# Two transformer blocks in one program: adaLN's shift left out of the first layer's h and added to k, v and the first queries as rows

## The reference, cut to what matters

```python
shift, scale, gate = jnp.split(jax.nn.silu(c) @ ada_w[l] + ada_b[l], 3, axis=-1)
h = rmsnorm(x, norm_g[l]) * (1.0 + scale[:, None]) + shift[:, None]      # the same for ctx with c_ctx
q, k, v, up, uf, g = split_proj(h @ w_in[l])
q = apply_axial_rope(rmsnorm(q.reshape(B, N, N_HEADS, HEAD_DIM), q_norm_g[l]), cos, sin)   # k alike
att = latent_attention(q, k, v, kc, vc)        # 8 query heads, 2 key heads of 128; keys of ctx and x
out = merge_branches(att, up, uf, g, pool_w[l], pool_scale[l], fourier_w[l], w_out[l])
x_new = x + gate[:, None] * out
```

## Time and profile before

| | |
|---|---|
| median of 3 runs | 2457.78 us (2452.79 to 2459.43) |
| the profiled execution's own time | 2455.74 us |
| its span | 2453.9 us |
| PE busy | 2318.9 us, 94% |
| DVE busy | 1288.8 us, 53% |
| ACT busy | 1044.1 us, 43% |
| HBM read over the span | 428.37 MB |
| mean granted TensorE clock | 0.976 of 2.4 GHz |

### The profile page before, as it was taken

The page is one execution under the profiler, slowest core; times in us unless marked ns, Lnnn a source line. Parts: engine busy times, 40 slices in busy tenths (PEclk is TensorE's granted clock), DMA queues, the critical chain, the costliest instruction groups (busy, mean ns, idle before and its releaser), DMA issues.

```text
span 2453.9 us, 30582 instructions
## 1 busy us (share of the span) xinstructions
PE 2318.9 (94%) x12135; PEld 1857.9 (76%) x12135; DVE 1288.8 (53%) x2110; ACT 1044.1 (43%) x1596; POOL 196.6 (8%) x237
## 2 busy tenths in 40 slices
PE   5889999999999997899998988989999999999998
PEld 2467777777777665678887877868888888888887
DVE  2444533132332254445666786556765666566664
ACT  2232333342321263445544555445543555345543
POOL 1000100000010122100012014120000000000001
PEclk8989999999999998999999999989999999999999
DMA  9764343435655583534555554545555555566652
GB/s 367 284 246 163 131 140 108 138 104 172 240 172 172 183 302 114 188 105 141 186 172 155 175 186 129 173 135 187 184 189 185 184 186 187 190 188 188 195 187 89
DMA packets 347021, 436.66 MB, mean 178 GB/s; under 512 B 13848, under 2 KB 269280, under 8 KB 345984
## 3 DMA queue, kind: packets, MB, share of 16 engines
q1 hardware_dynamic: 341376, 413.19, 51.1%
q0 software_dynamic: 3408, 16.38, 1.8%
q10 hardware_dynamic: 2096, 5.15, 0.6%
HBM read 428.37 MB, written 6.29 MB: 177 GB/s over the span
## 4 chain that ended last, share of the span: by engine, by line
PE 84%; DVE 5%; ACT 4%; DMA 3%; POOL 2%; issue 2%; SPq 0%; ACTq 0%; POOLq 0%; DVEq 0%
PE ps L1142 31%; PE ps L1143 16%; PE ps L1137 5%; PE ps L1139 5%; PE ps L1138 5%; PE ps L1123 4%; PE ps L1125 4%; PE ps L1124 4%; PE ps L1104 3%; ACT SPL L1320 2%; DMA RAW<-in_w_in_dram 2%; DVE SPL L1546 1%; PE ps L1187 1%; PE ps L1204 1%; DMA RAW<-in_ada_w_dram 1%
## 5 line engine op out<-in xcount | busy, mean ns | idle before, releaser
L1142 PE MATMUL ps<-HS,SPL 128*128 128x512 f32 x3456 | 1230.0, 401 | 18.0 <-POOL HS L1998 17.0
L1546 DVE TENSOR_TENSOR SPL<-RAW,SPL 128x1024 fp32r<-128x1024 f32 x592 | 725.7, 1231 | 667.2 <-ACT SPL L1320 665.6
L1143 PE MATMUL ps<-HS,SPL 128*128 128x256 f32 x3456 | 968.8, 280 | 0.0
L1320 ACT ACTIVATE SPL<-RAW 128x1024 fp32r<-128x1024 f32 x592 | 621.8, 1057 | 538.1 <-PE ps L1143 349.6
L1142 PEld LDWEIGHTS ps<-HS,SPL 128*128 128x128 f32 x3456 | 654.3, 189 | 182.3 <-POOL HS L1998 17.6
L1143 PEld LDWEIGHTS ps<-HS,SPL 128*128 128x128 f32 x3456 | 656.6, 190 | 2.1 <-issue 1.9
L1123 PE MATMUL ps<-SPL,HS 128*128 128x512 f32 x576 | 248.0, 430 | 22.3 <-ACT XT L1362 8.6
L1125 PE MATMUL ps<-SPL,HS 128*128 128x512 f32 x576 | 228.3, 396 | 0.0
L1124 PE MATMUL ps<-SPL,HS 128*128 128x512 f32 x576 | 228.1, 396 | 0.0
L1137 PE MATMUL ps<-HS,SPL 128*128 128x512 f32 x512 | 212.3, 415 | 1.2 <-DVE HS L1702 1.2
L1139 PE MATMUL ps<-HS,SPL 128*128 128x512 f32 x512 | 200.5, 392 | 0.0
(11 more groups left out here) (251 smaller groups left out, 1542.0 us busy)
## 6 DMA issues: line engine op xcount, KB each, us to landing
RAW<-in_w_in_dram SPq DMA_DIRECT2D x208, 512.0 KB, 5.7
RAW<-in_ada_w_dram SPq DMA_DIRECT2D x192, 512.0 KB, 4.9
RAW<-in_ffn_w_up_dram SPq DMA_DIRECT2D x192, 512.0 KB, 3.5
RAW<-in_w_out_dram SPq DMA_DIRECT2D x96, 512.0 KB, 4.5
RAW<-in_ffn_w_down_dram SPq DMA_DIRECT2D x96, 512.0 KB, 3.3
x_spill<-XT POOLq DMA_DIRECT2D x2, 2048.0 KB, 15.1
XT<-x_spill POOLq DMA_DIRECT2D x1, 4096.0 KB, 16.1
MM<-in_x_dram ACTq DMA_DIRECT2D x2, 1024.0 KB, 10.6
```

The source lines that it names most:

```text
L1142: mm(PS[b][:, :], wr, hh, start=k == 0, stop=False, skip_group_check=True)
L1143: m = mm(PS[b][:, 256:512], wl, hh[:, 0:256], start=False, stop=k == KT - 1, skip_group_check=True)
L1320: act(SPL[:, (n - 1) % NSPL, 0, :], raw_of(i), ACT.Copy).then_inc(s_hi, 1)
L1546: tt(w[:, 1, :], raw_of(s["i"]), w[:, 0, :].bitcast(F32), ALU.subtract).then_inc(s_lo, 1)
```

## The change

Layer 0 reads k, v and the first queries from an h without the shift (`bare`), which needs only the scale groups. `start(u)` has 8 adaLN chunks (40 chunks in all with k,v instead of 72), and in u = 0 each second of them pops six steps. The shift groups come with q0 (`go_on(u)`), and `shift_h` then adds the shift to h in place (DVE, ACT, DVE), ahead of q1 and all that follows. The rows of k,v and q0 are copied from PSUM into BARE, in MM. What the shift contributes to them, shift @ w_in, is computed by itself: the w_in columns of k,v and of q0 are loaded once more as 16 chunks of form "ada", multiplied by ADA's shift columns, copied, spread over the 128 rows by a matmul with a selecting matrix (`shift_rows`, SPREAD, loaded by `select_in`), and added by DVE. q0's norm steps are made after that, behind q1's in the list, and the low list of attention rows starts there. `mixed` places pairs of `left` chunks after every chunk of the output stage and after every two elsewhere. AHEAD is 7 (from chunk 40 on). In layer 1 q0 and q1 have side 2, their norm steps go to the front of `hi` and through bank 7, and q1's rows no longer flush the list.

```diff
...
-AHEAD = 5
+AHEAD = 7
...
+        BARE = [MV[:, i, 8:16, :].rearrange("p k n -> p (k n)").rearrange("p (t c) -> p t c", t=4) for i in range(2)]
+        SPREAD = MV[:, 1, 7, :].rearrange("p (v n) -> p v n", v=2)
...
-            while at["taken"] < min(len(queue), at["pos"] + (START_AHEAD if at["pos"] < 72 else at["ahead"])):
+            while at["taken"] < min(len(queue), at["pos"] + (START_AHEAD if at["pos"] < 40 else at["ahead"])):
...
-                    pop_side(2 if c.group.side == 2 and c.kc % 2 == 0 else 0)
+                    pop_side(c.group.side if c.kc % 2 == 0 else 0)
...
-        def mixed(main, left):
+        def mixed(main, left, every=2):
             seq = []
-            for c in main:
-                seq.append(c)
-                if len(seq) % 4 == 2:
-                    seq.extend(left[:2])
-                    del left[:2]
+            for i in range(0, len(main), every):
+                seq.extend(main[i:i + every] + left[:2])
+                del left[:2]
             return seq
...
+        def shift_h(k, s, bare, done, used):
+            y = {}
+            def s0():
+                y["slot"], last = take()
+                y["h"] = put("h0", l=0, k=k, s=s, slot=y["slot"], shifted=True, last=[ada_ready[0, k // 4], bare[k, s], *last])["n"]
+            def s1():
+                y["h"] = put("h1", l=0, k=k, s=s, slot=y["slot"], scaled=y["h"], last=[used])["n"]
+            def s2():
+                h = put("h2", l=0, k=k, s=s, slot=y["slot"], hi=y["h"], again=0)
+                give(y["slot"], (s_h2, h["n"]))
+                done[k, s] = (s_h2, h["n"])
+            return [s0, s1, s2]
...
-                if both or x.get("qs_used"):
+            def rows_out(banks, width, queries=False):
+                if queries and not both:
+                    while x.get("norms_left"):
+                        hi.pop(0)()
+                elif x.get("qs_used"):
                     flush(hi)
                 x["qs_used"] = True
-                s = put("rows_out", l=l, banks=banks, width=width, last=[multiplied(), *x["qs"]], a=count.get("qa", 0), d=count.get("qd", 0))
-                x["qs"] = []
+                while "tab" not in x:
+                    hi.pop(0)()
+                last, x["qs"] = [multiplied(), *x["qs"]], []
+                return copy_rows(banks, width, [lv.QS[:, i, 0:width] for i in range(len(banks))], last)
...
+            def bare_out(which):
+                def f():
+                    x["bare"][which] = copy_rows([0, 1, 2, 3], 512, [BARE[which][:, i, :] for i in range(4)], [multiplied()])
+                return f
+            def shift_rows(which):
+                def after():
+                    slot, last = take()
+                    s = put("ada_out", slot=slot, last=[multiplied(), *last])
+                    bank_last[6] = [(s_adaE, s["n"])]
+                    if not hi:
+                        hi.append(idle)
+                    hi.insert(1, lambda: add(slot, s["n"]))
+                def add(slot, out):
+                    while "scr_a" not in x:
+                        hi.pop(0)()
+                    s = put("shift_rows", which=which, slot=slot, out=out, ready=x["bare"][which], last=x["scr_a"], after=use(4, 5))
+                    n = 4 * s["n"]
+                    give(slot, (s_sp, s["n"]))
+                    bank_last[4], bank_last[5] = [(s_srow, n)], [(s_srow, n)]
+                    if which == 0:
+                        hi.extend(staged([norm_item(i, 2, 1, tt, (s_srow, n - 3 + i), lv.KTr[:, :, i * 128:(i + 1) * 128], BARE[0][:, i, 0:256])
+                                          for i, tt in enumerate(TILES)]))
+                    else:
+                        hi.extend(staged([norm_item(i, 4, 0, tt, (s_srow, n - 3 + i), MV[:, tt[0], 0:4, tt[1] * 128:(tt[1] + 1) * 128], BARE[1][:, i, :])
+                                          for i, tt in enumerate(TILES)]) + [lambda: start_units(0)])
+                return group("ada", "shift", W, (1024, 0)[which], [6], after)
...
-                    ready = rows_out(banks, 512)
-                    hi.extend(staged([norm_item(i, 4, 0, tt, ready[i], MV[:, tt[0], 4 * g:4 * g + 4, tt[1] * 128:(tt[1] + 1) * 128])
-                                      for i, tt in enumerate(lv.tiles)]))
-
-                    def start_units():
-                        us.extend(unit(hd, *tt) for hd in range(4 * g, 4 * g + 4) for tt in lv.tiles)
-                        if g == 0 and both:
-                            low.extend([unit_row] * (2 * len(us) + 3))
-                    hi.append(start_units)
+                    ready = rows_out(banks, 512, True)
+                    steps = staged([norm_item(i, 4, 0, tt, ready[i], MV[:, tt[0], 4 * g:4 * g + 4, tt[1] * 128:(tt[1] + 1) * 128])
+                                    for i, tt in enumerate(lv.tiles)]) + [lambda: start_units(g)]
+                    if both:
+                        hi.extend(steps)
+                    else:
+                        x["norms_left"] = True
+                        hi[:0] = steps + [lambda: x.update(norms_left=False)]
                 return f
+            def start_units(g):
+                us.extend(unit(hd, *tt) for hd in range(4 * g, 4 * g + 4) for tt in lv.tiles)
+                if g == 0 and both:
+                    low.extend([unit_row] * (2 * len(us) + 3))
...
-            kv = group("tm", ("kv", l), W, 1024, [0, 1, 2, 3], kv_out, TILES)
-            q0 = group("tm", ("in", l), W, 0, qb[0], q_out(0, qb[0]), lv.tiles)
-            q1 = group("tm", ("in", l), W, 512, qb[1], q_out(1, qb[1]), lv.tiles)
+            kv = group("tm", ("kv", l), W, 1024, [0, 1, 2, 3], bare_out(0) if both else kv_out, TILES)
+            q0 = group("tm", ("kv", l), W, 0, qb[0], bare_out(1), TILES) if both else group("tm", ("in", l), W, 0, qb[0], q_out(0, qb[0]), lv.tiles, 1 if both else 2)
+            q1 = group("tm", ("in", l), W, 512, qb[1], q_out(1, qb[1]), lv.tiles, 1 if both else 2)
...
-                cs = ada_group(0, 4 + u, 2) + ada_group(0, u, 2)
+                cs = ada_group(0, 4 + u, 2 if u else 6)
                 after_ada = cs[-1].then
                 def start_h():
                     after_ada()
                     if u == 3:
                         put("spill", last=[multiplied()])
-                    hi.extend(staged([tile_h(0, k, s, x, h) for k in range(4 * u, 4 * u + 4) for s in range(2)])
-                              + ([load_tables, tables, load_dft] if u == 3 else []))
+                    hi.extend(staged([tile_h(0, k, s, x, bare) for k in range(4 * u, 4 * u + 4) for s in range(2)])
+                              + ([lambda: put("select_in"), load_tables, tables, load_dft] if u == 3 else []))
                 cs[-1].then = start_h
-                return cs[:12] + kv[2 * u - 2:2 * u - 1] + cs[12:] + kv[2 * u - 1:2 * u] if u else cs
+                return cs[:4] + kv[2 * u - 2:2 * u - 1] + cs[4:] + kv[2 * u - 1:2 * u] if u else cs
+            def go_on(u):
+                c = q0[2 * u + 1]
+                after_q = c.then
+                def add_shift():
+                    while (0, u) not in ada_ready:
+                        hi.pop(0)()
+                    used = multiplied()
+                    hi.extend(staged([shift_h(k, s, bare, h, used) for k in range(4 * u, 4 * u + 4) for s in range(2)]))
+                    if after_q:
+                        after_q()
+                c.then = add_shift
+                cs = ada_group(0, u, 2)
+                return cs[:4] + q0[2 * u:2 * u + 1] + cs[4:] + [c]
...
-                main = [c for u in range(4) for c in start(u)] + kv[6:8], q0 + q1 + gp + gf + gates
+                main = ([c for u in range(4) for c in start(u)] + kv[6:8] + [c for u in range(4) for c in go_on(u)]
+                        + mixed(q1, shift_rows(0) + shift_rows(1), 1)), gp + gf + gates
...
-        lay_out(mixed(outs0, left))
+        lay_out(mixed(outs0, left, 1))
...
+                elif kind == "shift_rows":
+                    for sm, v in new((s_sel, 16)):
+                        e.wait_ge(sm, v)
+                    e.wait_ge(s_adaE, s["out"])
+                    for src in range(2):
+                        m = mm(PS[4 + src][:, :], SPREAD[:, src, :], T(s["slot"]), start=True, stop=True, skip_group_check=True)
+                    m.then_inc(s_sp, 1)
...
+                    if s["shifted"]:
+                        stt(T(s["slot"])[:, 0:256], HX(0, k, src, 0).bitcast(F32), shift(0, k, src), HX(0, k, src, 1).bitcast(F32), ALU.add, ALU.add).then_inc(s_h0, 1)
+                        continue
...
-                    stt(HX(0, k, src, 1), T(s["slot"])[:, 0:256], shift(0, k, src), HX(0, k, src, 0).bitcast(F32), ALU.add, ALU.subtract).then_inc(s_h2, 1)
+                    tt(HX(0, k, src, 1), T(s["slot"])[:, 0:256], HX(0, k, src, 0).bitcast(F32), ALU.subtract).then_inc(s_h2, 1)
+                elif kind == "shift_rows":
```

(21 more changed lines are left out.)

76 lines of the change are left out of this document (45 added, 31 removed).

## The result

The changed kernel takes 2501.44 us (median of 4 runs, 2495.56 to 2505.73) against 2458.56 us of the kernel before (4 runs). The ratio is 1.0173, interval 1.0156 to 1.019: 42.9 us slower, where 12 us faster was predicted.

What follows compares the result with a forecast made beforehand. TensorE, busy 94% of the span, was taken as the bound. Start -13.6, attention burst +9.8 and layer 1 -8 summed to -11.8 us, 2446 us (own range 2440 to 2453; eight times in ten 2428 to 2464).

Steps and rivals of the forecast that it cites:

- (a): Layer 0's start: first wide matmul at 47.5 us, 18.8 us sooner, with half as many adaLN chunks ahead.
- (b): Layer 0, first wide matmul to end of k,v: ends at 106 us, the 8.3 us spill wait gone.
- (c): Layer 0's q0 with the shift's 32 adaLN chunks: 61.3 us of PE plus 7 of waits, ending at 174.5 us.
- (d): Layer 0's q1 with 16 shift chunks: 54.4 us of work plus 6 of waits, ending at 235 us.
- Seven chunks ahead where no adaLN chunk stands changes nothing: Deeper split look-ahead where no adaLN chunk stands: priced at 0, as four splits are the limit.
- (e): Layer 0's pool group: second spread 1.7, q0's transposes 2.3 and 4 us of waits, reaching 243 us.
- (f): Start's like-for-like correction for gate chunks (8 us) and attention rows (11 us) now later: 262 against 275.6, -13.6 us.
- Attention burst: Layer 0's third gate group: 13 attention rows run in a row without wide matmuls, +9.8 us (bounds 0 to 45).
- Layer 1: Layer 1's start: q1 -12 us from shorter head-transpose waits, q0 +4, together -8 us (bounds -18 to +2).
- The adaLN chunks moved into the output stage are the same work: 0: Layer 0's output stage: a pair and wide chunk take 6.4 us of PE against 4.3 of loads, no change.
- Rival (2): No change, some 2456 us: table waits, norm waits and slower loads give back 15.5 us at full; chance 0.25 with another.
- Rival (1): Slower: attention burst without overlap, deciding the sign from 1.7 us idle a row; 2475 us at 3 us; chance 0.15.

Runs made afterwards that it cites:

- e8: Changed kernel with the gate group needing heads 0 and 1 two groups later, splits five chunks ahead up to chunk 136 and seven after: 2454.5 us.
- e13: e7 with the splits seven chunks ahead from chunk 40 up to chunk 136, five behind it: 2480.4 us.
- e1: Changed kernel with the splits five chunks ahead instead of seven: 2471.4 us, ratio to before 1.006.
- e7: e5 with 16 adaLN chunks moved back from layer 0's output stage to layer 1's start: 2440.3 us, ratio to before 0.9923.
- e9: e7 with layer 1's own steps undone as well: 2448.1 us.
- e2: Changed kernel with the gate group that needs heads 0 and 1 put two groups later: 2488.2 us.
- e5: Changed kernel with e1 and e2 together, splits five ahead and gate group later: 2455.8 us, ratio to before 0.999.
- e10: Kernel before the change with the change's layer 1 steps alone: 2454.6 us, ratio to before 0.9983.

## Why the prediction was wrong, step by step

- **(a), (b) First wide matmul and k,v: right.** 44.9 us for 47.5, 106.1 for 106. The 8.3 us wait of the earlier trace rows is gone.
- **(c), (d) q0 and q1: right for five ahead, wrong for the kernel as it is.** With five ahead q0 ended at 170.8 to 174.6 us (predicted 174.5) and q1 at 230.9 to 233.1 (235). In the changed kernel it was 192.3 and 261.3. (VectorE's wait for the rope tables was 6.3 us there, against the 10.5 of the earlier trace rows.) The step that failed is the sentence "Seven chunks ahead where no adaLN chunk stands changes nothing, as four splits are the limit: 0". It priced the depth only where no adaLN chunk stands; but in q0 and q1 adaLN chunks stand between all w_in chunks. Up to the end of the Fourier group it costs 33 to 36 us (e8, e13, e1), and 30 to 40 in the medians. I never asked what is queued behind a split that waits for its load.
- **(e), (f) The start's gain: right with five ahead.** e7 and the kernel before have done the same work at the end of the output stage, with 24 adaLN chunks left for layer 1 in both, and e7 has read its 16 chunks twice by then. It is there at 839.0 us, e9 at 842.0, the kernel before at 853.5: 11.5 to 14.5 us sooner, where I had 13.6.
- **Attention burst: place and mechanism right, size a third short.** +9.8 predicted; 13.3 (e2) and 15.7 us (e5 against e1) measured. Of the 13.8 us in e2's output stage 11.0 are idle and 2.7 busy time of PE, which I had left out.
- **Layer 1: q1's -12 right (-12.3), q0 +7.6 instead of +4.** Together -4 to -5 instead of -8 (e9, e10), within a scatter of some 6 us, and only with 24 adaLN chunks in place.
- **"The adaLN chunks moved into the output stage are the same work: 0": wrong by 15.5 us (e7).** The work is the same, but layer 1 did it in waits, and the output stage has none.

The sum as measured: start -11.5 to -14.5, seven ahead +30, burst +13 to +16, the 16 moved chunks +15.5, layer 1 about 0 without them: +44 to +50 against +42.9. The rest is within the scatter, or the parts overlap by some us. Rival (2) had named the direction, late norms in (d) and waits in (c), but priced them at 15.5 us at full, and not by the depth. Rival (1), the one for slower, was wrong: a burst row cost 1.0 to 1.2 us (13.3 and 15.7 us over 13 rows), not the 1.7 from which it decides.

## What to carry to other kernels

A look-ahead is not free on an in-order engine: ask, for every chunk that it reaches further, when its load can start and which short steps stand behind it in the queue. Filler work belongs in stages where the bounding engine waits; "the same work elsewhere" is only neutral between two stages with equal idle time. When a change has several parts, time each part's undoing: here three parts that cost 30, 13 and 15 us hid a start whose gain was predicted within some 2 us. And look at where a difference stands: a stage that the edit doesn't touch can differ by 6 us from one execution to the next.

## What the runs showed of the hardware

Two adaLN chunks read as 1.07 us of matmuls in the timeline, and I counted 1.00 us, but they lengthen a stream of wide matmuls by 1.22 us. With both streams loading, q0 moved 341 GB/s at a share of 0.96 (e1), between the 322 and 364 GB/s that I had weighed. Behind a wait of PE of 3.5 us matmuls were 0.43 us apart instead of 0.23 for some 5 us. In the burst, with no wait longer than 2.1 us but 4.2 us idle between 520 and 530 us, the clock also fell, to 0.51 and 0.64 in the two slices of 2 us behind that wait; a mean of 0.97 over 60 us had hidden it. The same 6256 matmuls of the second block were busy 1120.4 us in one execution (e5) and 1132.4 in another (e9), at mean clocks of 0.98 and 0.97, with the same idle time.
